# A mixture-of-experts kernel: five experts in the 128-row form and three in the 64-row form, where there were four and four

## The chip, the core and the metric

The kernel runs on one core of one Trainium2 chip. The metric is device time in microseconds (us) of one execution; the kernel before takes 2024.12 us, the median of three runs (2022.58 to 2025.73). All arithmetic is fp32. A product that has to be accurate to fp32 is made of cheaper products of parts: each operand is split into a high part (rounded to `float32r`, by a copy) and a low part (what the rounding left, by a subtraction).

## The reference

Two blocks run one after the other on a sequence of 256 tokens with 1024 features. The first has three attention branches and a feed-forward; the second has two layers, the last of which ends in a mixture of experts. The change touches only this last part:

```
logits = h @ w_router                      # 8 experts
top_val, top_idx = lax.top_k(logits, 2)    # each of 256 tokens goes to 2 experts
gates = softmax(top_val)
y_e = (silu(x_e @ w_gate[e]) * (x_e @ w_up[e])) @ w_down[e]   # x_e: the tokens of expert e
out = sum over the 2 experts of gates * y_e
```

Each expert has gate and up matrices of 1024 by 3584 and a down matrix of 3584 by 1024, 44 MB together, so 352 MB for the eight.

## The kernel before

The mixture runs expert by expert, in eight positions, 0 to 7. All weights stream through four slots of 2 MB each (three in `ring`, one in `ring4`), 21 loads per expert, issued by the SyncE queue in `sp_program`; `load` waits until the last piece of the slot's earlier load has been split. Each load is split in two pieces: ScalarE copies a piece to its high part (`split_to` in `act_program`, line 1180), VectorE subtracts to get the low part (`split_to` in `dve_program`, line 1749), into four pairs of buffers (WHB and WLB, WHX and WLX). TensorE then multiplies, and a buffer is free again when TensorE has read it.

An expert's 3584 hidden columns are done in seven chunks of 512, grouped by `steps_of` as (0), (1, 2), (3, 4), (5, 6); the last expert has (0, 1), (2, 3), (4, 5), (6). In each step come the gate pieces, the up pieces, and then the down pieces of the step before (`expert_piece`, `expert_down`). The tokens of an expert are picked by a product with a 0/1 matrix PO (`lists`, `gather`), and its output is put back by another (`combine`). So the down products of an expert's last two chunks stand behind the gate and up of the next expert's chunk 0.

There are two forms of expert, chosen by position:

- **heavy** (128 rows): the tokens' high parts lie in EH, the low parts in EL. Every product takes three matmuls, high by high, high by low and low by high (`mm3`, lines 426 to 428). One turn per chunk is four transposes (line 1036).
- **light** (64 rows): high and low parts lie side by side in the 128 columns of EH, so two matmuls do the same (lines 1008 and 1009 for gate and up, 1054 and 1055 for down). The turn adds the halves and takes 16 small matmuls per chunk (line 1032).

`order` in `dve_program` ranks the experts by how many tokens they got, most first, with expert 0 always at rank 0 because its loads start before the routing is known. RANK says which rank each position takes; EID, the ids in order of rank, is read by the SyncE queue for the addresses of the loads. CAPV is each expert's limit of tokens, 128 for the ranks that are heavy and 64 for the others. If any expert has more than its limit, a second pass (`sp_second`, `pe_second` and others) loads all the weights once more.

Before the change the positions are heavy, light, heavy, light, heavy, light, heavy, light. The order of the work on each engine is fixed when the program is built; engines wait for each other by semaphores.

Of the kernel before, what the change touches and what calls it, by code (L numbers as in the profile page):

```python
# [12 lines left out]
ALU = mybir.AluOpType  # L13
# [7 lines left out]
NE = 8  # L21
# [7 lines left out]
LIM = 128  # L29
LIM_L = 64  # L30


RANK = (0, 4, 1, 5, 2, 6, 3, 7)
LIGHT = (1, 3, 5, 7)
HEAVY = NE - len(LIGHT)


def steps_of(ex):
# [84 lines left out]
def build(nc, I, table, out):  # L123
    ctx = ExitStack()
    with ctx:
# [98 lines left out]
        def sm(n):  # L224
            sm_at[0] += n
            assert sm_at[0] <= 1008
            return SM[:, sm_at[0] - n:sm_at[0]]
# [180 lines left out]
        def pe_program(e):  # L408
# [3 lines left out]
            def room(b):  # L412
                if banks.last[b] is not None:
                    pe.wait_ge(*banks.last[b])
# [555 lines left out]
            def gather(ex, q):  # L970
# [3 lines left out]
                pe.wait_ge(s_hl, 2)  # L974
                light = ex in LIGHT
                for n, src in enumerate((HH, HL)):
# [14 lines left out]
            def expert_piece(kind, ex, cs, k):  # L991
# [3 lines left out]
                at_ = 0 if kind == "gate" else 2  # L995
                if ex not in LIGHT:
                    pe.wait_ge(*banks.out["ga", ex, (k // 2 if two else k), 0])
                pe.wait_ge(*banks.out["ga", ex, (k // 2 if two else k), 1])
                n_kt = 2 if two else 4
                for j in range(n_kt):  # L1000
                    kt = n_kt * k + j
                    for x, c in enumerate(cs):
# [3 lines left out]
                        wh, wl = hi[:, j, CH * x:CH * x + CH], lo[:, j, CH * x:CH * x + CH]  # L1006
                        if ex in LIGHT:
                            e.matmul(PS[b][:, :], EH[:, kt, :], wh, start=(kt == 0), stop=False)  # L1008
# [13 lines left out]
            def expert_turn(ex, c):  # L1022
                n = NCH * ex + c
                i = n % 2
                room(6)
                if ex in LIGHT:
                    pe.wait_ge(s_tab2, 16)
# [11 lines left out]
            def expert_down(ex, c):  # L1039
                i = (NCH * ex + c) % 2  # L1040
                for h2 in range(2):
# [5 lines left out]
                    for jj in range(2):  # L1047
                        j = 2 * h2 + jj
                        xs = slice(128 * j, 128 * j + 128)
                        for q in range(2):  # L1050
                            cs = slice(512 * q, 512 * q + 512)
                            first, end = c == 0 and j == 0, c == NCH - 1 and j == 3
                            if ex in LIGHT:
                                e.matmul(PS[4 + q][:, :], HTH[:, i, xs], hi[:, jj, cs], start=first, stop=False)  # L1054
# [9 lines left out]
            def scatter_lists(ex):  # L1064
# [3 lines left out]
                for tt in range(2):  # L1068
                    e.transpose(PS[7][:, 128 * tt:128 * tt + 128], PO[:, tt, :].bitcast(F32), ident)
                r = RANK[ex]  # L1070
                e.matmul(PS[7][:, 256:257], PO[:, 0, :].bitcast(F32), GR[:, 0, r:r + 1], start=True, stop=False)
# [666 lines left out]
        def dve_program(e):  # L1738
            v = Stream(e, s_dve)
# [210 lines left out]
            for i, w in enumerate((WFG, WRT)):  # L1950
                t = v.step(e.tensor_copy(W8[2 * i][:, :, :], w[:, :, :]))
# [143 lines left out]
            t = v.step(e.tensor_tensor(LBM, L3[:, 0, :], L3[:, 1, :], ALU.max))  # L2095
            v.wait_ge(*t)
            t = v.step(e.tensor_tensor(LBM, LBM, L3[:, 2, :], ALU.max))
# [3 lines left out]
            t = v.step(e.tensor_tensor(LBS, E3[:, 0, :], E3[:, 1, :], ALU.add))  # L2101
            v.wait_ge(*t)
            t = v.step(e.tensor_tensor(LBS, LBS, E3[:, 2, :], ALU.add))
            v.wait_ge(*t)
            t = v.step(e.reciprocal(LBS, LBS))
            v.wait_ge(*t)
            t = v.step(e.tensor_tensor(LB, E3[:, 0, :], LBS, ALU.mult))
# [54 lines left out]
            t = v.step(e.tensor_tensor_scan(flat(CC), flat(RM), flat(LF), 0.0, ALU.mult, ALU.add))  # L2162
# [20 lines left out]
            for tt in range(2):  # L2183
                for g in range(2):
                    v.wait_ge(s_osq, 2 * tt + g + 1)
                    t = v.step(e.tensor_reduce(SS_HG[:, 8 * tt + 4 * g:8 * tt + 4 * g + 4], SQ2[:, tt, 512 * g:512 * g + 512].rearrange("p (h d) -> p h d", h=4), AX.X, ALU.add))
# [3 lines left out]
            for tt in range(2):  # L2190
                for g in range(2):
                    r = root(("hg", tt))
                    ov = OR[:, tt, 512 * g:512 * g + 512]
                    t = banks.out["ho", tt, g]
# [22 lines left out]
            t = v.step(e.tensor_tensor(LP.rearrange("p (a d) -> p a d", a=2), L4[:, :, 0, :], L4[:, :, 1, :], ALU.mult))  # L2217
# [3 lines left out]
            t = v.step(e.tensor_tensor(NL, LE[:, 1:2], LE[:, 0:1], ALU.subtract))  # L2221
# [96 lines left out]
            for tt in range(2):  # L2318
# [3 lines left out]
                t = v.step(e.tensor_tensor(Q4[:, tt], oth, own, ALU.is_equal))  # L2322
                v.wait_ge(*t)
                t = v.step(e.tensor_tensor(Q4[:, tt], Q4[:, tt], tri, ALU.mult))
# [4 lines left out]
            t = v.step(e.tensor_reduce(MK, C4, AX.X, ALU.add))  # L2329
# [12 lines left out]
            def lists(ex):  # L2342
# [6 lines left out]
                for tt in range(2):  # L2349
                    t = e.tensor_scalar(PO[:, tt, :], iota, pos[:, tt, RANK[ex]:RANK[ex] + 1], None, ALU.is_equal)  # L2350
                t.then_inc(s_po, 1)

            def order():

                v.wait_ge(s_one, 2)
                t = v.step(e.memset(NCNT[:, 0:1], 999.0))
                v.wait_ge(*t)
                oth = NCNT.unsqueeze(1).to_broadcast([128, 8, 8])
                own = NCNT.unsqueeze(2).to_broadcast([128, 8, 8])
                v.step(e.tensor_tensor(C4[:, 0], oth, own, ALU.is_gt))  # L2360
                t = v.step(e.tensor_tensor(C4[:, 1], oth, own, ALU.is_equal))
                v.wait_ge(*t)
                t = v.step(e.tensor_tensor(C4[:, 1], C4[:, 1], tri, ALU.mult))
                v.wait_ge(*t)
                t = v.step(e.tensor_tensor(C4[:, 0], C4[:, 0], C4[:, 1], ALU.add))
                v.wait_ge(*t)
                t = v.step(e.tensor_reduce(RNK, C4[:, 0], AX.X, ALU.add))
                v.wait_ge(*t)
                t = v.step(e.tensor_scalar(CAPV, RNK, HEAVY - 0.5, float(LIM - LIM_L), ALU.is_lt, ALU.mult))
                eight = CT[:, C_IOTA:C_IOTA + 8]  # L2370
                t2 = v.step(e.tensor_tensor(C4[:, 0], RNK.unsqueeze(1).to_broadcast([128, 8, 8]), eight.unsqueeze(2).to_broadcast([128, 8, 8]), ALU.is_equal))
                v.wait_ge(*t)
                t = v.step(e.tensor_scalar(CAPV, CAPV, float(LIM_L), None, ALU.add))
                v.wait_ge(*t2)
                t2 = v.step(e.tensor_tensor(C4[:, 1], C4[:, 0], eight.unsqueeze(1).to_broadcast([128, 8, 8]), ALU.mult))
                v.wait_ge(*t2)
                t2 = v.step(e.tensor_reduce(MX8[:, 0, :], C4[:, 1], AX.X, ALU.add))
                v.wait_ge(*t2)
                e.tensor_copy(EID[:, :], MX8[0:1, 0, :]).then_inc(s_perm, 1)
                v.wait_ge(*t)  # L2380
                v.wait_ge(s_rte, 2)
                for src, dst in ((POS, POSR), (G, GR)):
                    if src is G:
                        v.wait_ge(s_gw, 2)
                    for tt in range(2):
                        t = v.step(e.tensor_tensor(Q4[:, tt], C4[:, 0], src[:, tt, :].unsqueeze(1).to_broadcast([128, 8, 8]), ALU.mult))
                    v.wait_ge(*t)
                    for tt in range(2):
                        t = e.tensor_reduce(dst[:, tt, :], Q4[:, tt], AX.X, ALU.add)
                    if src is G:  # L2390
                        t.then_inc(s_gw, 1)
                    else:
                        v.wait_ge(*v.step(t))
                t = v.step(e.tensor_tensor(MX8[:, 1, :], CNT0, CAPV, ALU.subtract))
                v.wait_ge(*t)
                t = v.step(e.tensor_reduce(MOST, MX8[:, 1, :], AX.X, ALU.max))
                v.wait_ge(*t)
                e.tensor_scalar(CNT[:, :], MOST[0:1, :], float(LIM), None, ALU.add).then_inc(s_most, 1)
# [54 lines left out]
            t = v.step(e.tensor_scalar(H[:, :, :], H[:, :, :], ALPHA, None, ALU.mult))  # L2453
# [4 lines left out]
            t = v.step(e.tensor_scalar(E2, E2, 1.0, None, ALU.add))  # L2458
            v.wait_ge(*t)
            t = v.step(e.reciprocal(E2, E2))  # L2460
            v.wait_ge(*t)
            for tt in range(2):
                e.scalar_tensor_tensor(out=G[:, tt, :], in0=LG8[:, tt, :], scalar=E2[:, tt:tt + 1], in1=MK[:, tt, :], op0=ALU.mult, op1=ALU.mult).then_inc(s_gw, 1)
            order()
            before = []
            for ex in range(NE):
# [251 lines left out]
        def sp_program(e):  # L2718
            q = Stream(e, s_pe)

            def source(i):
# [5 lines left out]
                if ex and (kind, at_) == ("gate", (0, 0)):  # L2727
                    q.wait_ge(s_perm, 1)
                    T["expert", ex] = e.value_load(EID[0:1, RANK[ex]:RANK[ex] + 1], min_val=0, max_val=NE - 1)
                w = w[bass.ds(T["expert", ex], 1)] if ex else w[0:1]  # L2730
# [46 lines left out]
        def flat(x):  # L2777
            return x.rearrange("p h n -> p (h n)")
# [56 lines left out]
        NCNT, CNT0, RNK, CAPV = sm(8), sm(8), sm(8), sm(8)  # L2835
# [71 lines left out]
```

## Time and profile before

| what | value |
|---|---|
| median of three runs | 2024.12 us (2022.58 to 2025.73) |
| the profiled execution | 2025.73 us, its span 2023.9 us |
| TensorE, share of the span busy | 94% |
| VectorE, ScalarE | 74%, 60% |
| HBM read | 509.05 MB |
| experts' loads | 56 of gate, 56 of up, 56 of down, 2 MB each |

The span is the time from the first to the last recorded instruction. The mixture starts at about 1081 us, when the first gather runs, and holds the rest of the span. Because the experts repeat one pattern, the best reading is by windows cut at the same place of each expert: here from the last down matmul of one expert to that of the next, which on TensorE fall at about 1219.4, 1325.9, 1446.4, 1553.1, 1673.6 and 1779.9 us. These five windows are the experts at positions 1 to 5. Each holds chunk 0's gate and up of the expert that follows, and not those of its own, which stand in the window before.

### The profile page before, as it was taken

To read this page: it belongs to the slowest core of one execution; us is meant where nothing else is said; L and a number is where in the kernel's file an instruction comes from. 1 tells how busy PE (TensorE), PEld (TensorE's weight loads), DVE (VectorE), ACT (ScalarE), POOL (GpSimd) and SP (SyncE) were. 2 spreads that over 40 slices of the span, in tenths; PEclk is the share of its full clock that TensorE was granted. 3 is DMA by queue.
4 is the path that set the end of the run, shared out by engine and by line. 5 is a ranking of instruction groups with operands and counts; after the bars stand their busy time and mean duration, and the time that the engine had idled before them with its cause. 6 is when DMAs were issued, how large, how long until landed. Compare 5 with 4: busy or idle time off the path is not lost.

```text
span 2023.9 us, 22529 instructions
## 1 busy us (share of the span) xinstructions
PE 1897.2 (94%) x9235; PEld 1560.2 (77%) x9235; DVE 1501.0 (74%) x1431; ACT 1212.2 (60%) x1243; POOL 156.8 (8%) x123
## 2 busy tenths in 40 slices
PE   5999999999998899989878999999999999999994
PEld 4778777888987778877566887788878887788873
DVE  4645456544589754466667889998999989998996
ACT  4554435433563444344435778877888778877883
POOL 1301010000133210031101000000000000000000
PEclk9999999999999999999877999999999999999997
DMA  8433334554532455444234999999999999999992
GB/s 278 145 134 137 125 125 166 208 177 147 187 136 84 146 207 188 145 163 150 83 132 172 381 355 394 409 406 368 362 414 406 377 363 396 409 405 367 372 409 84
DMA packets 154317, 511.62 MB, mean 253 GB/s; under 512 B 4334, under 2 KB 8672, under 8 KB 139872
## 3 DMA queue, kind: packets, MB, share of 16 engines
q1 hardware_dynamic: 151888, 502.91, 65.7%
q0 software_dynamic: 1424, 4.59, 0.8%
q10 hardware_dynamic: 896, 2.62, 0.3%
q8 instruction: 75, 1.23, 0.2%
q14 instruction: 34, 0.28, 0.0%
HBM read 509.05 MB, written 1.05 MB: 252 GB/s over the span
## 4 chain that ended last, share of the span: by engine, by line
PE 72%; DVE 17%; DMA 4%; ACT 3%; issue 3%; POOL 1%; DVEq 0%; SPq 0%; ACTq 0%; POOLq 0%
PE PS L426 19%; PE PS L428 19%; PE PS L427 19%; DVE WLB L1749 6%; DVE WLX L1749 5%; DMA ring<-in_moe_w_down 3%; PE PS L1054 1%; PE PS L1055 1%; ACT WHB L1180 1%; PE PS L987 1%; PE PS L929 1%; DMA ring<-in_w_mem_kv 1%; PE PS L559 1%; DVE AR L2136 1%; PE PS L840 1%
## 5 line engine op out<-in xcount | busy, mean ns | idle before, releaser
L1749 DVE TENSOR_TENSOR WLB<-ring,WHB 128x2048 fp32r<-128x2048 f32 (+1 forms) x344 | 647.6, 1898 | 136.8 <-ACT WHB L1180 136.2
L1180 ACT ACTIVATE WHB<-ring 128x2048 fp32r<-128x2048 f32 (+1 forms) x344 | 534.1, 1561 | 349.6 <-PE PS L428 315.1
L1749 DVE TENSOR_TENSOR WLX<-ring,WHX 128x2048 fp32r<-128x2048 f32 (+1 forms) x216 | 467.6, 2189 | 49.7 <-ACT WHX L1180 49.6
L1180 ACT ACTIVATE WHX<-ring 128x2048 fp32r<-128x2048 f32 (+1 forms) x216 | 393.3, 1837 | 158.4 <-PE PS L428 137.1
L426 PE MATMUL PS<-WHB,XH 128*128 128x512 f32 (+1 forms) x640 | 258.0, 403 | 11.8 <-DVE XL L1800 6.8
L428 PE MATMUL PS<-WHB,XL 128*128 128x512 f32 (+1 forms) x640 | 251.2, 393 | 0.0
L427 PE MATMUL PS<-WLB,XH 128*128 128x512 f32 (+1 forms) x640 | 250.8, 392 | 0.0
L426 PEld LDWEIGHTS PS<-WHB,XH 128*128 128x128 f32 x640 | 123.2, 192 | 38.0 <-issue 11.4
L2575 POOL TENSOR_TENSOR SM<-SM,MH 128x8 f32<-128x8 f32 (+3 forms) x28 | 36.2, 1299 | 1451.7 <-DVE SM L1762 1451.7
L428 PEld LDWEIGHTS PS<-WHB,XL 128*128 128x128 f32 x640 | 122.8, 192 | 26.2
L427 PEld LDWEIGHTS PS<-WLB,XH 128*128 128x128 f32 x640 | 123.0, 192 | 23.8
L426 PE MATMUL PS<-WHX,XH 128*128 128x512 f32 (+1 forms) x240 | 92.3, 384 | 4.7 <-DVE WLX L1749 4.7
L1008 PE MATMUL PS<-WHB,EH 128*128 128x512 f32 x224 | 91.0, 406 | 2.9 <-DVE WLB L1749 2.0
L428 PE MATMUL PS<-WHX,XL 128*128 128x512 f32 (+1 forms) x240 | 91.4, 381 | 0.0
L427 PE MATMUL PS<-WLX,XH 128*128 128x512 f32 (+1 forms) x240 | 91.3, 381 | 0.0
L1008 PE MATMUL PS<-WHX,EH 128*128 128x512 f32 x224 | 89.9, 401 | 0.3
L426 PE MATMUL PS<-WHX,EH 128*128 128x512 f32 x224 | 89.2, 398 | 0.0
L426 PE MATMUL PS<-WHB,EH 128*128 128x512 f32 x224 | 88.5, 395 | 0.0
L426 PE MATMUL PS<-WHB,HTH 128*128 128x512 f32 x224 | 87.9, 392 | 0.0
L428 PE MATMUL PS<-WHB,EL 128*128 128x512 f32 x224 | 87.8, 392 | 0.0
L427 PE MATMUL PS<-WLB,EH 128*128 128x512 f32 x224 | 87.7, 391 | 0.0
L428 PE MATMUL PS<-WHX,EL 128*128 128x512 f32 x224 | 87.7, 391 | 0.0
(398 smaller groups left out, 3538.7 us busy)
## 6 DMA issues: line engine op xcount, KB each, us to landing
ring<-in_moe_w_gate SPq DMA_DIRECT2D x56, 2048.0 KB, 10.5
ring<-in_moe_w_up SPq DMA_DIRECT2D x56, 2048.0 KB, 11.0
ring<-in_moe_w_down SPq DMA_DIRECT2D x56, 2048.0 KB, 11.0
ring<-in_w_in SPq DMA_DIRECT2D x13, 2048.0 KB, 8.1
ring<-in_hg_w_in SPq DMA_DIRECT2D x8, 2048.0 KB, 8.4
ring<-in_da_w_in SPq DMA_DIRECT2D x6, 2048.0 KB, 8.1
ring<-in_w_gate SPq DMA_DIRECT2D x5, 2048.0 KB, 8.7
ring<-in_w_up SPq DMA_DIRECT2D x5, 2048.0 KB, 7.8
```

The source lines that it names most:

```text
L426: e.matmul(o, xh, wh, start=start, stop=False)
L427: e.matmul(o, xh, wl, start=False, stop=False)
L428: return e.matmul(o, xl, wh, start=False, stop=stop)
L559: e.matmul(PS[2][:, a0:a1], q_[o:o + 64, j, 128 * qt:128 * qt + 128], k_[o:o + 64, j, 0:n], start=True, stop=False)
L840: t = e.matmul(PS[b][:, 128 * j:128 * j + 128], a_k[:, h, 128 * s_t:128 * s_t + 128], a_q[:, h, 128 * t_t:128 * t_t + 128], start=True, st ...
L929: e.matmul(PS[b][:, a0:a1], QD[o:o + 64, h, 128 * qt:128 * qt + 128], KD[o:o + 64, h, 0:n], start=True, stop=False)
L987: t = e.matmul(PS[b][:, 128 * j:128 * j + CAP], src[:, tt, 128 * d:128 * d + 128], PO[:, tt, :], start=(tt == 0), stop=(tt == 1))
L1008: e.matmul(PS[b][:, :], EH[:, kt, :], wh, start=(kt == 0), stop=False)
L1054: e.matmul(PS[4 + q][:, :], HTH[:, i, xs], hi[:, jj, cs], start=first, stop=False)
L1180: e.activation(hi, src, ACT.Copy).then_inc(s_hi, 1)
L1749: e.tensor_tensor(lo, src, hi.bitcast(F32), ALU.subtract).then_inc(s_lo, 1)
L2575: e.tensor_tensor(RR[name], RV[name], MH[:, 0:RR[name].shape[1]], ALU.pow).then_inc(s_rs, 1)
```

## The change

Two tables and one constant are edited. Positions 1, 4 and 7 are now light (1, 3, 5, 7 before), so the order of forms is heavy, light, heavy, heavy, light, heavy, heavy, light. RANK is permuted so that the five heavy positions take ranks 0 to 4 and the three light ones 5, 6 and 7. The comparison that gives each expert its limit of tokens has 4.5 in place of HEAVY - 0.5, which was 3.5, and the name HEAVY is gone.

```diff
-RANK = (0, 4, 1, 5, 2, 6, 3, 7)
-LIGHT = (1, 3, 5, 7)
-HEAVY = NE - len(LIGHT)
+RANK = (0, 5, 1, 2, 6, 3, 4, 7)
+LIGHT = (1, 4, 7)
...
-                t = v.step(e.tensor_scalar(CAPV, RNK, HEAVY - 0.5, float(LIM - LIM_L), ALU.is_lt, ALU.mult))
+                t = v.step(e.tensor_scalar(CAPV, RNK, 4.5, float(LIM - LIM_L), ALU.is_lt, ALU.mult))
```

Since one line is gone, every line number of the changed kernel behind it is one lower. The first place is TensorE where position 2 (heavy) hands over to position 3. Before, EH and HTH are high parts of tokens and hidden values, and PO is the 0/1 matrix; the gather is in the light form:

```order
L426 MATMUL PS<-WHB,EH 128x512
L427 MATMUL PS<-WLB,EH 128x512
L428 MATMUL PS<-WHB,EL 128x512
L985 MATMUL PS<-PO,XH 128x64 x8
L985 MATMUL PS<-PO,XL 128x64 x8
L426 MATMUL PS<-WHX,HTH 128x512
```

In the changed kernel the same place reads:

```order
L425 MATMUL PS<-WHB,EH 128x512
L426 MATMUL PS<-WLB,EH 128x512
L427 MATMUL PS<-WHB,EL 128x512
L986 MATMUL PS<-PO,XH 128x128 x8
L986 MATMUL PS<-PO,XL 128x128 x8
L425 MATMUL PS<-WHX,HTH 128x512
```

The gather has the same number of matmuls and moves 128 columns in each instead of 64. A little later, where chunk 0 of position 3 starts, each weight tile was used twice before:

```order
L427 MATMUL PS<-WLB,HTH 128x512
L428 MATMUL PS<-WHB,HTL 128x512
L1008 MATMUL PS<-WHX,EH 128x512
L1009 MATMUL PS<-WLX,EH 128x512
L1008 MATMUL PS<-WHX,EH 128x512
```

and is now used three times:

```order
L426 MATMUL PS<-WLB,HTH 128x512
L427 MATMUL PS<-WHB,HTL 128x512
L425 MATMUL PS<-WHX,EH 128x512
L426 MATMUL PS<-WLX,EH 128x512
L427 MATMUL PS<-WHX,EL 128x512
```

Over the whole program TensorE gets 168 matmuls of 128x512 more (8088 after 7920), 60 of 128x128 more (1525 after 1465) and 88 of 128x64 fewer (312 after 400).

The second engine is VectorE, at the same handover from position 2 to position 3. Before, after the list PO of the next expert, it splits pieces (WLB, WLX) and finishes two products of gate and up (HID):

```order
L2350 TENSOR_SCALAR PO<-CT,SM 128x128 x2
L1749 TENSOR_TENSOR WLB<-ring,WHB 128x2048
L2420 TENSOR_TENSOR HTL<-PS,HTH 128x512
L1749 TENSOR_TENSOR WLX<-ring,WHX 128x2048 x2
L2427 TENSOR_TENSOR HID<-PS,HID 128x512 x2
L1749 TENSOR_TENSOR WLB<-ring,WHB 128x2048 x2
L1749 TENSOR_TENSOR WLX<-ring,WHX 128x2048 x2
```

Now two copies of the tokens' low parts to EL stand between the splits:

```order
L2349 TENSOR_SCALAR PO<-CT,SM 128x128 x2
L1748 TENSOR_TENSOR WLB<-ring,WHB 128x2048
L2419 TENSOR_TENSOR HTL<-PS,HTH 128x512
L1748 TENSOR_TENSOR WLX<-ring,WHX 128x2048 x2
L2426 TENSOR_TENSOR HID<-PS,HID 128x512 x2
L1748 TENSOR_TENSOR WLB<-ring,WHB 128x2048
L2405 CAST EL<-PS 128x512
L1748 TENSOR_TENSOR WLB<-ring,WHB 128x2048
L1748 TENSOR_TENSOR WLX<-ring,WHX 128x2048
L2405 CAST EL<-PS 128x512
```

The order of the loads in the SyncE queue is the same; only the expert that a position's loads fetch is another one.

## Rows read from the trace of the kernel before

**Rows 1.** The page: share of busy time, TensorE's granted clock and bandwidth in 40 slices.

```profile
PE 1897.2 (94%) x9235; PEld 1560.2 (77%) x9235; DVE 1501.0 (74%) x1431; ACT 1212.2 (60%) x1243; POOL 156.8 (8%) x123
...
PEclk9999999999999999999877999999999999999997
...
GB/s 278 145 134 137 125 125 166 208 177 147 187 136 84 146 207 188 145 163 150 83 132 172 381 355 394 409 406 368 362 414 406 377 363 396 409 405 367 372 409 84
```

**Rows 2.** Windows, positions 1 to 5: us, then PE, PEld, DVE, ACT, POOL, clock, DMA.

```profile
1219.40:1325.90 106.50, 103.16 (x512) 84.01 (x511) 102.36 (x69) 90.43 (x73) 0.00 (x0) 1.00 1.02 402
1325.90:1446.40 120.50, 120.50 (x563) 100.64 (x562) 108.23 (x67) 89.93 (x62) 0.00 (x0) 1.00 0.98 376
1446.40:1553.10 106.70, 103.34 (x513) 84.04 (x512) 102.24 (x69) 90.47 (x73) 0.00 (x0) 1.00 1.02 404
1553.10:1673.60 120.50, 120.50 (x563) 100.65 (x562) 108.23 (x67) 89.93 (x62) 0.00 (x0) 1.00 0.97 375
1673.60:1779.90 106.30, 103.03 (x511) 83.88 (x510) 102.21 (x69) 90.56 (x73) 0.00 (x0) 1.00 1.02 404
```

**Rows 3.** Groups by line, PE, window of position 2 (heavy): xcount, busy us, mean ns, idle.

```profile
L426 PE MATMUL PS<-WHX,EH 128*128 128x512 f32 x48 | 19.2, 400 | 0.0
...
L426 PE MATMUL PS<-WHB,HTH 128*128 128x512 f32 x32 | 12.6, 393 | 0.0
...
L1036 PE MATMUL PS<-CT,HID 128*128 128x128 f32 x28 | 4.4, 280 | 0.0
...
L985 PE MATMUL PS<-PO,XL 128*128 128x64 f32 x16 | 2.1, 277 | 0.0
```

**Rows 4.** Groups by line, PE, window of position 3 (light).

```profile
L1008 PE MATMUL PS<-WHB,EH 128*128 128x512 f32 x48 | 19.8, 413 | 0.9 <-DVE WLB L1749 0.7
...
L1032 PE MATMUL PS<-CT,UB 128*128 128x64 f32 x56 | 7.7, 281 | 0.0
...
L987 PE MATMUL PS<-PO,XH 128*128 128x128 f32 x16 | 2.1, 273 | 1.1 <-DVE HTH L2417 1.1
```

**Rows 5.** Timeline of PE: start us, us, instruction. Heavy turn; then light matmuls and turn.

```profile
1328.64 0.63 PE L1036 MATMUL PS<-CT,HID 128*128 128x128 f32 x4
...
1329.34 0.39 PE L427 MATMUL PS<-WLB,EH 128*128 128x512 f32 x1
...
1446.47 0.39 PE L1008 MATMUL PS<-WHX,EH 128*128 128x512 f32 x1
...
1448.29 1.04 PE L1032 MATMUL PS<-CT,HID 128*128 128x64 f32 x8
...
1450.40 0.39 PE L1009 MATMUL PS<-WLX,EH 128*128 128x512 f32 x1
```

**Rows 6.** Windows, halves of the heavy position 2, then of the light position 3.

```profile
1326.00:1372.00 46.00, 46.00 (x210) 38.16 (x209) 42.77 (x26) 35.07 (x26) 0.00 (x0) 1.00 1.01 403
1372.00:1446.00 74.00, 74.00 (x353) 62.06 (x352) 64.96 (x40) 54.76 (x37) 0.00 (x0) 1.00 0.95 360
1446.00:1470.00 24.00, 23.14 (x105) 17.88 (x104) 23.23 (x16) 21.18 (x17) 0.00 (x0) 1.00 1.00 379
1470.00:1553.00 83.00, 80.50 (x410) 66.44 (x409) 79.31 (x55) 69.19 (x57) 0.00 (x0) 1.00 1.02 411
```

**Rows 7.** Waits in the heavy window of position 2: us in total, times, longest.

```profile
ACT WHX L1180 <- PE PS L428: 14.0, 16, 2.2
...
SPq L2744 <- DVE WLB L1749: 54.1, 11, 6.8
```

**Rows 8.** Waits in the light window of position 3.

```profile
PEld PS L1008 <- DVE WLB L1749: 2.9, 5, 1.1
...
ACT WHB L1180 <- DMA ring<-in_moe_w_up: 2.9, 2, 1.5
```

**Rows 9.** The page: one line's weight loads; issues of the gate weights.

```profile
L426 PEld LDWEIGHTS PS<-WHB,XH 128*128 128x128 f32 x640 | 123.2, 192 | 38.0 <-issue 11.4
...
ring<-in_moe_w_gate SPq DMA_DIRECT2D x56, 2048.0 KB, 10.5
```

## The prediction

> **What bounds the kernel now.** I read the page first, then windows cut expert by expert, then the groups by line inside one heavy and one light window, then the waits of the same two.
>
> The page [rows 1] shows TensorE busy 94% of the span and, from slice 23 on, a bandwidth that swings between 355 and 414 GB/s. That swing is the experts. The changed part alone decides, since nothing before 1081 us is edited.
>
> The five windows [rows 2] show two regimes. A window of a heavy position followed by a light one lasts 120.5 us twice, and TensorE is busy in all 120.50 us of both. A window of a light position followed by a heavy one lasts 106.5, 106.7 and 106.3 us; there TensorE has gaps of some 3.3 us, and VectorE is busy 102.24 of 106.7 us. The granted clock is 1.00 (the level of 2.4 GHz) in all five.
>
> That TensorE is busy is not yet a bound, because its matmuls overlap. The pitch is what to read. In the light stretch eight matmuls of 128x512 start from 1446.47 to 1448.29 us, when the turn starts [rows 5]: 1.82 / 8 = 0.2275 us each, though each one's own duration is about 0.39 us. The heavy window can be rebuilt from that pitch. It has 7 chunks x 24 positions x 3 = 504 matmuls for itself, less 16 x 3 for its own chunk 0, plus 16 x 2 for the light successor's: 488 x 0.2275 = 111.0. The turn costs 1329.34 - 1328.64 less one matmul = 0.47 us, seven times (28 transposes in [rows 3]) 3.3. That leaves 6.2 us for 32 gather matmuls, eight combine matmuls and the lists; the combine takes 8 x 0.2275 = 1.8. Nothing is left over for stalls. So a heavy expert goes at TensorE's issue pace.
>
> The other resources confirm it. In the heavy window ScalarE waits on TensorE's reads, 16 times for one pair of buffers [rows 7], and SyncE waits 54.1 us for slots behind one kind of piece alone. Once the slots have filled, the bandwidth falls from 403 to 360 GB/s [rows 6]. The transfers are ahead and idle for want of room.
>
> A light expert is bound elsewhere. After the stock of loads is used up its bandwidth is 411 GB/s [rows 6], ScalarE waits for the transfer and TensorE for the low parts of WLB [rows 8]. VectorE and the transfers share the bound there, TensorE has room. Its own sum is 352 x 0.2275 = 80.1 for the large matmuls, plus seven turns of 1450.40 - 1448.29 less one matmul = 1.88 us, 13.2, plus the same 6.2: 99.5 us against 106.5.
>
> **The change, part by part.**
>
> *One more heavy position.* Let a window end where the expert's last down matmul ends. Before, positions 1 to 5 give light-heavy 106.5, heavy-light 120.5, 106.7, 120.5, 106.3: 560.5 us. After, the pairs are light-heavy (1), heavy-heavy (2), heavy-light (3), light-heavy (4), heavy-heavy (5). Position 6 is heavy followed by the last light one as before, and position 0 is heavy followed by light as before, so both ends stay as they are.
>
> A heavy-heavy window does not occur in the trace. It is the heavy-light window with chunk 0's gate and up of its successor at three matmuls instead of two: 16 more, 16 x 0.2275 = 3.6 us. The gather of the successor is the same count at the same price, 277 ns a matmul for 64 columns [rows 3] and 273 for 128 [rows 4], so nothing. That makes 120.5 + 3.6 = 124.1 us.
>
> After: 106.5 + 124.1 + 120.5 + 106.5 + 124.1 = 581.7. The difference is 21.2 us, all of it on the path, because in heavy windows TensorE has no idle time at all.
>
> The same from the other side: 168 more matmuls of 128x512, 38.2 us; seven light turns replaced by heavy ones, -7 x (1.88 - 0.47) = -9.9; together 28.3 of issue. Of that, 7.0 us (106.5 - 99.5) was the light expert's waiting and small gaps, which vanish with it. 28.3 - 7.0 = 21.3. The two sums are not independent in the pitch but are in the windows; I take 21.3.
>
> *The handover heavy to heavy.* It brings two copies to EL on VectorE between the splits. Queued behind them are the next low parts, for which TensorE waits. VectorE is busy 108.23 of 120.5 us in a heavy window, so it has 12 us of slack for two copies under 0.7 us each, and between the two gathers TensorE now has 24 down matmuls (5.5 us) instead of 16 as cover. I take nothing. The bound above is what a heavy gather waits for after a light expert, 1.1 us [rows 4], twice: +2.2. The bound below is that the third matmul of chunk 0 is hidden, -3.6 twice: -7.3. The sum runs from 14.0 to 23.5.
>
> *What the slots pass on.* A heavy expert ends with its slots full; a second one cannot make them fuller. So the light expert after two heavy ones starts with the same stock as after one. I take nothing there.
>
> *Permuted ranks and the constant.* Same instructions, same loads; nothing. All 56 gate loads of [rows 9] are the first pass, so no expert overflows now. Limits only rise (rank 4 from 64 to 128), and the heavy positions take just the ranks 0 to 4, so no second pass appears.
>
> Two rules of the Trainium skill speak against this reading. Perfetto Trace Analysis, Identifying the Most-Contended Engine, says that matmul busy time is a bad measure of TensorE's headroom and LDWEIGHTS busy share a good one. Here that share is 100.64 / 120.50 = 84% in a heavy window [rows 2], and by the rule some 16% of it, 20 us, would be room in which the new matmuls could hide. The trace does not support it: one load takes 192 ns [rows 9], and 192 / 227.5 is 84% with no gap between matmuls, so 84% is this pattern's ceiling. SBUF — State Buffer, Summary: rules for kernel authors, says to plan with about 358 GB/s from HBM to SBUF; by that 44 MB would take 123 us for either form, and the change would cost nothing. The trace disagrees, with 411 GB/s in [rows 6].
>
> **The rivals.**
>
> *A, bytes set the pace.* All eight experts read the same 352 MB, so if transfers bound the whole stage, the form would not matter: 2024 us, no change. For it: 404 GB/s in light windows. Against it: 360 GB/s and waits for slots in the second half of a heavy one. Chance 2%.
>
> *A2, room on TensorE.* A heavy window has 120.50 - 100.64 = 19.9 us without a weight load. If the expert's third matmuls fitted in there, 1.4 us of cost would be left: 2025.5. For it: that share. Against it: the rebuilt window, in which the pitch of 0.2275 us leaves no gap. Chance 1%. The rule on the share of weight loads, above, is this case; the one on 358 GB/s is A.
>
> *B, the handover gives something back.* If chunk 0 of a heavy successor costs no more than that of a light one (the low end above), the cost is 14.0 us: 2038.1. For it: nothing measured heavy-heavy. Against: 100% busy at a fixed pitch. Chance 5%.
>
> *C, the light experts speed up.* This is the one that ends on the other side. Two heavy ones in a row give VectorE and the transfers time to get ahead; if the three light experts left then ran at TensorE's own sum, each would save 106.5 - 99.5 = 7.0, 21.0 together, and cancel the cost: 2024.4; with the gather's wait of 1.1 us gone in two of them as well, it would come out at 2022. It decides from the point where the stock at the start of a light expert exceeds today's. Against it: the slots are full after 46 us of a heavy expert [rows 6], and there are only four. Chance 2%.
>
> *D, the second pass appears* through a wrong limit: another 352 MB at 404 GB/s, about 870 us more. Chance below 1%.
>
> *E, dearer handovers*, beyond +2.2: something in the new order stalls TensorE, up to three times 1.1 us at each of the two, 2052. Chance 4%.
>
> **How the numbers follow.** The forecast has the remaining 86%. The profiled execution took 2025.73 us, 1.8 beyond its span, and would become 2047.0. The median shown is 2024.12, 1.6 below that execution, and the prediction is made against it: 2024.12 + 21.3 = 2045.4 us. Runs of before spread over 3.2 us. The range of the forecast with its bound above is 2043 to 2048; widened toward B and E it is 2040 to 2050, which leaves out A, A2, C, D and most of B and E. A measurement here can tell about 0.2%, 4 us, from no change: slower by more than that holds for the forecast, B and E, 95%; within it A, A2 and half of C, 3%; faster, the other half of C and what nobody thought of, 2%.
>
> **What would show it.** Right: windows cut at the last down matmul of about 106.5 at positions 1 and 4, 124.1 at 2 and 5, 120.5 at 3, TensorE busy throughout 2, 3 and 5, and 360 GB/s over nearly all of position 3. Wrong: a light window well below 106 (C), a heavy-heavy one of 120.5 (B) or above 127 (E), or gaps on TensorE inside 2, 3 and 5.

## The result and the profile after

| | median of its runs | profiled execution, span |
|---|---|---|
| before, timed beside it | 2024.92 us (2022.58 to 2027.77) | 2025.73, 2023.9 us |
| changed | 2044.62 us (2043.73 to 2046.56) | 2045.65, 2043.9 us |

The ratio is 1.0098, 95% interval 1.0081 to 1.0115: 19.7 us slower, 20.0 us between the spans. The forecast was 2045.4.

The lines of the changed kernel's page that answer to [rows 1]:

```profile
PE 1922.6 (94%) x9319; PEld 1583.1 (77%) x9319; DVE 1507.5 (74%) x1433; ACT 1211.3 (59%) x1229; POOL 158.2 (8%) x123
...
PEclk9999999999999899989778999999999999999997
...
GB/s 275 150 136 127 124 124 166 205 185 169 161 124 83 168 205 203 127 162 165 42 169 231 376 359 404 409 397 352 351 364 366 411 408 387 351 359 363 373 409 75
```

TensorE is busy 25.4 us longer and its share is 94% as before: a share of the whole span says nothing here. The bandwidth now stays at 351 to 366 GB/s for four slices in a row, where two heavy experts stand together.

The windows cut at the last down matmul of each expert say where the time went. This is the changed kernel, positions 1 to 6 and then the rest (us, then PE, PEld, DVE, ACT, POOL, clock, DMA share, GB/s):

```profile
1217.10:1323.50 106.40, 103.07 (x512) 83.97 (x511) 102.33 (x69) 90.58 (x73) 0.00 (x0) 1.00 1.02 405
1323.50:1447.70 124.20, 124.20 (x580) 103.72 (x579) 110.66 (x70) 89.91 (x61) 0.00 (x0) 1.00 0.97 371
1447.70:1568.20 120.50, 120.50 (x563) 100.64 (x562) 106.39 (x66) 89.61 (x61) 0.00 (x0) 1.00 0.95 361
1568.20:1674.00 105.80, 102.83 (x511) 83.97 (x510) 102.11 (x69) 90.40 (x73) 0.00 (x0) 1.00 1.02 404
1674.00:1798.20 124.20, 124.20 (x580) 103.72 (x579) 110.65 (x70) 89.87 (x61) 0.00 (x0) 1.00 0.97 371
1798.20:1927.40 129.20, 128.41 (x595) 106.40 (x594) 115.11 (x70) 97.46 (x66) 0.00 (x0) 1.00 0.96 361
1927.40:2043.90 116.50, 87.98 (x407) 69.11 (x405) 94.26 (x77) 70.91 (x61) 4.90 (x4) 0.87 0.66 264
```

and these are the last two windows of before, which [rows 2] does not hold:

```profile
1779.90:1909.20 129.30, 128.53 (x595) 106.47 (x595) 116.98 (x71) 97.74 (x67) 0.00 (x0) 1.00 0.97 376
1909.20:2023.90 114.70, 85.35 (x407) 67.65 (x405) 94.35 (x77) 70.78 (x61) 4.44 (x4) 0.91 0.66 267
```

Between the ends of the last down matmuls themselves (1217.39 and 1798.31 now, 1219.72 and 1780.11 before) windows 1 to 5 last 580.9 us and lasted 560.4: +20.5. Window 6 has not moved. The rest is 1.8 us longer, at a lower granted clock (0.87 after 0.91); the first edge comes 2.3 us earlier, though the work in front of it is the same. 20.5 + 1.8 - 2.3 = 20.0.

In window 2, which has no counterpart before, ScalarE waits on TensorE's reads even oftener than in [rows 7], and SyncE waits for slots:

```profile
ACT WHX L1179 <- PE PS L427: 16.4, 19, 2.2
...
SPq L2743 <- DVE WLB L1748: 56.1, 11, 6.4
```

and its gate and up products stand in groups of 56 where [rows 3] has 48, six of them, so 48 matmuls for the successor's chunk 0:

```profile
L425 PE MATMUL PS<-WHB,EH 128*128 128x512 f32 x56 | 21.9, 391 | 0.0
```

### The profile page after: what moved, and what is told of

The parts are those of the page before. It is cut to its first block, busy times and chain, and to the rows that moved or that the text cites. A ratio compares the mean times of both kernels' runs of the same rounds, so it can differ in the third digit from the quotient of the medians.

```text
span 2043.9 us, 22687 instructions
## 1 busy us (share of the span) xinstructions
PE 1922.6 (94%) x9319; PEld 1583.1 (77%) x9319; DVE 1507.5 (74%) x1433; ACT 1211.3 (59%) x1229; POOL 158.2 (8%) x123
## 4 chain that ended last, share of the span: by engine, by line
PE 75%; DVE 14%; DMA 4%; ACT 3%; issue 2%; POOL 1%; DVEq 0%; SPq 0%; ACTq 0%; POOLq 0%
PE PS L425 21%; PE PS L427 21%; PE PS L426 21%; DVE WLB L1748 4%; DVE WLX L1748 4%; DMA ring<-in_moe_w_down 3%; PE PS L986 1%; PE PS L1053 1%; PE PS L1054 1%; DMA ring<-in_w_mem_kv 1%; PE PS L928 1%; PE PS L558 1%; ACT WHB L1179 1%; PE PS L1035 1%; DVE AR L2135 1%
## 5 line engine op out<-in xcount | busy, mean ns | idle before, releaser
L425 PE MATMUL PS<-WHB,EH 128*128 128x512 f32 x280 | 111.1, 397 | 0.0
L425 PE MATMUL PS<-WHX,EH 128*128 128x512 f32 x280 | 110.9, 396 | 0.0
L427 PE MATMUL PS<-WHB,EL 128*128 128x512 f32 x280 | 109.7, 392 | 0.0
L427 PE MATMUL PS<-WHX,EL 128*128 128x512 f32 x280 | 109.4, 391 | 0.0
L426 PE MATMUL PS<-WLB,EH 128*128 128x512 f32 x280 | 109.4, 391 | 0.0
L426 PE MATMUL PS<-WLX,EH 128*128 128x512 f32 x280 | 109.0, 389 | 0.0
L425 PE MATMUL PS<-WHB,HTH 128*128 128x512 f32 x240 | 94.3, 393 | 0.0
L427 PE MATMUL PS<-WHB,HTL 128*128 128x512 f32 x240 | 93.5, 390 | 0.0
L426 PE MATMUL PS<-WLB,HTH 128*128 128x512 f32 x240 | 93.4, 389 | 0.0
```

The costliest lines, as they stand in the source:

```text
L425: e.matmul(o, xh, wh, start=start, stop=False)
L426: e.matmul(o, xh, wl, start=False, stop=False)
L427: return e.matmul(o, xl, wh, start=False, stop=stop)
```

## The experiments

The theory to test: a heavy expert costs what TensorE needs to issue it, whatever its neighbours are; a light one costs what VectorE (or the transfers) need. So form, not place, decides a heavy one's price. The median of before drifts between sessions (2024.9 to 2028.3 us), so I compare ratios to before and, above all, windows. A line of a diff that starts or ends with `...` is shortened.

**Six heavy experts.** One heavy more than the change.

```diff
-RANK = (0, 5, 1, 2, 6, 3, 4, 7)
-LIGHT = (1, 4, 7)
+RANK = (0, 6, 1, 2, 3, 4, 5, 7)
+LIGHT = (1, 7)
...
-... e.tensor_scalar(CAPV, RNK, 4.5, ...
+... e.tensor_scalar(CAPV, RNK, 5.5, ...
```

Expected: 

> Six heavy positions and two light: heavy, light, five heavy in a row, light. Theory (a heavy expert costs TensorE's issue pace, whatever stands before it): against the changed kernel one light-heavy and one heavy-light window (106.3 + 120.5) become two heavy-heavy ones (2 x 124.2), so 2044.6 + 21.6 = 2066 us, and no window differs from these sizes. Rival (heavy experts in a row give the light ones a better start, or queue up something): the last light expert's share from 1927.4 us to the end, 116.5 us, gets shorter, or the later heavy windows get longer than 124.2.

Measured: 2066.94 us, ratio 1.0205 (1.0184 to 1.0226), after 1.0098: 1.07%, 21.7 us. All four heavy-heavy windows take 124.1 us; two of them:

```profile
1449.10:1573.20 124.10, 124.10 (x579) 103.66 (x578) 108.75 (x69) 89.64 (x60) 0.00 (x0) 1.00 0.94 355
...
1697.40:1821.50 124.10, 124.10 (x579) 103.65 (x578) 108.73 (x69) 89.64 (x60) 0.00 (x0) 1.00 0.93 355
```

The price is the same for the next heavy expert. A heavy expert with four heavy ones around it is as fast as one of two. The light window at position 1 took 108.6 us, at a granted clock of 0.98 (see the last section). The last light expert's stretch took 113.8 us (116.5 in the changed kernel, 114.7 before), which one could read as a better start after five heavy ones. But from the edge to the end of TensorE's last long wait it took 83.8 us in both this and the changed kernel; the difference lies in the 16 down matmuls behind that wait, and there it is the clock (last section).

**Two matmuls in place of three at the handover.** Chunk 0 of positions 3 and 6 leaves out the tokens' low parts, so the changed kernel's two heavy-heavy windows hold 16 matmuls fewer each.

```diff
-                        if ex in LIGHT:
+                        if ex in LIGHT or ex in (3, 6) and cs == (0,):
                             e.matmul(PS[b][:, :], EH[:, kt, :], wh, start=(kt == 0), stop=False)
```

Expected: 

> The changed kernel, but in chunk 0 of the heavy experts at positions 3 and 6 (the successors in the two heavy-heavy windows) gate and up take two matmuls instead of three: it leaves out the product of the tokens' low parts there. 2 x 16 matmuls of 128x512 fewer. Theory: 2 x 3.6 = 7.3 us faster than the changed kernel, 2037.3, both heavy-heavy windows at 120.5 instead of 124.1. Rival (the third matmul hides behind splits, weight loads or transfers): no change, windows stay at 124.1.

Measured: 2038.74 us, ratio 1.0063 (1.0039 to 1.0087). 0.35% under the change is 7.1 us, though the two intervals just overlap; the windows are what decides. Both fall from 124.2 to 120.5:

```profile
1323.20:1443.70 120.50, 120.50 (x564) 100.66 (x563) 109.49 (x69) 89.47 (x61) 0.00 (x0) 1.00 0.96 371
1670.50:1791.00 120.50, 120.50 (x563) 100.67 (x562) 109.45 (x69) 89.52 (x61) 0.00 (x0) 1.00 0.98 375
```

Sixteen matmuls fewer save 3.6 us in each, 0.226 us a matmul: each is paid with its pitch and nothing hides. Rival B and rival A2 have fallen.

**Half the bytes for the heavy experts.** Each load of positions 2, 3, 5 and 6 fetches the first half only and leaves old values in the rest of the slot, so the output is not the layer's; the same edit with `in LIGHT` serves the two kernels with half loads below.

```diff
-                e.dma_start(slot(i)[:, 0:t * n].rearrange("p (t n) -> p t n", t=src.shape[1]), src).then_inc(s_ring[SLOT[i]], 16)
+                dst = slot(i)[:, 0:t * n].rearrange("p (t n) -> p t n", t=src.shape[1])
+                if WL[i][2] is None and int(WL[i][0].split()[1]) in (2, 3, 5, 6):
+                    dst, src = dst[:, 0:dst.shape[1] // 2, :], src[:, 0:src.shape[1] // 2, :]
+                e.dma_start(dst, src).then_inc(s_ring[SLOT[i]], 16)
```

Expected: 

> The changed kernel, but each weight load of the heavy experts at positions 2, 3, 5 and 6 brings only half of its bytes, 88 MB less in all (the other half of a slot keeps old values). Theory (heavy experts are bound by TensorE, and their slots are full long before their end anyway): no change, within 1 us, windows 124.1, 120.5, 124.1. Rival A (bytes set the pace): 88 MB at 404 GB/s are 218 us; even a tenth of it would be 22 us faster.

Measured: 2042.51 us, ratio 1.0082 (1.0054 to 1.0111), which overlaps the change's. Two of the windows:

```profile
1320.70:1444.90 124.20, 124.20 (x580) 103.73 (x579) 110.66 (x70) 89.91 (x61) 0.00 (x0) 1.00 0.53 184
1444.90:1565.40 120.50, 120.50 (x563) 100.62 (x562) 106.40 (x66) 89.61 (x61) 0.00 (x0) 1.00 0.63 227
```

At 184 GB/s instead of 371 not a tenth of a microsecond is gained. For the heavy windows rival A has fallen; the light ones are the next question. The profiled span is still 5.5 us shorter than the change's, where I expected at most 1: 3.3 of it lie before the first edge, which the edit does not reach, and 3.0 behind position 6, while windows 1 to 5 are together 0.8 longer.

**Half the bytes for the light experts** of the changed kernel.

Expected: 

> The changed kernel, but each weight load of the light experts (positions 1, 4, 7) brings only half of its bytes. It asks whether a single light expert between heavy ones is bound by VectorE or by bytes. VectorE: its windows of 106.3 and 105.8 us stay within 0.5 us, and only the last one, which has no heavy expert behind it, may gain 1 to 2. Bytes: the windows fall to TensorE's own sum of 99.5 us, 6 to 7 us each, some 15 to 20 us in all.

Measured: 2039.04 us, ratio 1.0060 (1.0040 to 1.0080), 0.38% under the change. The windows of positions 1 and 4:

```profile
1215.60:1321.00 105.40, 102.80 (x512) 83.92 (x511) 101.84 (x69) 90.45 (x73) 0.00 (x0) 1.00 0.71 253
1565.70:1671.10 105.40, 102.74 (x511) 83.96 (x510) 101.84 (x69) 90.46 (x73) 0.00 (x0) 1.00 0.70 253
```

They get 1.0 and 0.4 us shorter, the first by more than my 0.5 but neither by 6 to 7, so bytes do not bind a light expert between heavy ones. TensorE's own sum of 99.5 us is not reached either. What is left is VectorE, busy 101.84 of 105.40 us: every wait of TensorE in the window of position 4 that ends on another engine ends on a VectorE result, mostly a low part, and none on a transfer. The largest group is

```profile
PEld PS L1007 <- DVE WLX L1748: 2.9, 5, 1.1
```

No run took work off VectorE, so this last step is read from the trace and not shown by an edit.

Behind position 6, 116.5 us became 112.5, more than I expected (1 to 2). Of the 4.0 us, 1.4 are the clock in the last 16 down matmuls (last section). The other 2.6 lie in the 83.8 us in front of them; but half the bytes for the heavy experts, with the last expert's own loads whole, shows 2.0 of them as well, so I cannot call them bytes.

**The same four and four, in two groups.** Heavy at 0 to 3, light at 4 to 7.

```diff
-RANK = (0, 5, 1, 2, 6, 3, 4, 7)
-LIGHT = (1, 4, 7)
+RANK = (0, 1, 2, 3, 4, 5, 6, 7)
+LIGHT = (4, 5, 6, 7)
...
-... e.tensor_scalar(CAPV, RNK, 4.5, ...
+... e.tensor_scalar(CAPV, RNK, 3.5, ...
```

Expected: 

> Four heavy and four light as before the change, but in two groups: heavy at positions 0 to 3, light at 4 to 7. Three heavy-light and three light-heavy windows of before become three heavy-heavy (124.2) and three light-light. Theory V (a light expert is bound by VectorE: busy 102.24 us plus 4.6 us of handoffs in a window of 106.7): a light-light window has no copies to EL and no heavy product of the successor, 106.5 - 2.7 = 103.8 us, so +3 x (3.7 - 2.7) = +3 us against before, 2028. Theory B (without a heavy neighbour to refill the slots, light experts are bound by bytes: 44.04 MB at 411 GB/s = 107.2 us): +3 x (3.7 + 0.7) = +13 us, less up to 3 that the first one takes from full slots, 2035 to 2038.

and the same with half the bytes for its light experts. Expected: 

> The kernel with heavy experts at positions 0 to 3 and light ones at 4 to 7, and each weight load of a light expert brings only half of its bytes (the other half of the slot keeps old values). Theory V (VectorE bounds light experts): like the same kernel with full loads, within 1 us each, about 2028. Theory B (bytes): 9 to 10 us faster than with full loads, light-light windows fall from 107 to VectorE's 103.8.

Measured: 2036.54 us, ratio 1.0059 (1.0037 to 1.0081), and with half the bytes 2025.29, ratio 0.9999 (0.9989 to 1.0009). Here is grouping with full loads, light windows 4, 5 and 6:

```profile
1588.10:1693.30 105.20, 101.76 (x496) 81.81 (x494) 100.09 (x66) 89.25 (x74) 0.00 (x0) 0.98 1.02 405
1693.30:1800.10 106.80, 101.45 (x494) 80.45 (x494) 102.34 (x67) 90.95 (x75) 0.00 (x0) 1.00 1.02 411
1800.10:1917.50 117.40, 110.89 (x526) 87.59 (x526) 111.30 (x71) 99.23 (x79) 0.00 (x0) 0.99 1.02 411
```

and with half loads:

```profile
1588.80:1691.00 102.20, 99.46 (x496) 80.69 (x494) 99.77 (x66) 90.38 (x74) 0.00 (x0) 1.00 0.62 208
1691.00:1796.30 105.30, 101.91 (x494) 81.81 (x495) 102.09 (x67) 91.22 (x75) 0.00 (x0) 0.98 0.61 210
1796.30:1909.80 113.50, 109.96 (x526) 87.69 (x526) 110.92 (x71) 99.41 (x81) 0.00 (x0) 0.98 0.61 213
```

Grouping costs 0.59%, 12 us, and with half the bytes all of that is gone. Not all of it need be the grouping's: half loads for three light experts of the changed kernel gave 0.38% too, mostly behind position 6. But here the windows themselves shrink, and with full loads ScalarE waits 15.5 us for transfers in window 5, with half loads not at all. So theory B holds for light experts in a row: without a heavy neighbour that refills the slots, 411 GB/s is the pace, 106.8 us in the first window without a stock (107.2 expected). Between heavy ones VectorE is the pace. The earlier experiment and this one agree: the same expert has two bounds, by its neighbours. The windows account for 3.0, 1.5 and 3.9 us of the 9.7 between the two spans; the second and third half-load windows have a granted clock of 0.98, so they are no clean measure of VectorE's pace.

**Three heavy experts.** Heavy at 0, 3 and 6; run twice.

```diff
-RANK = (0, 5, 1, 2, 6, 3, 4, 7)
-LIGHT = (1, 4, 7)
+RANK = (0, 3, 4, 1, 5, 6, 2, 7)
+LIGHT = (1, 2, 4, 5, 7)
...
-... e.tensor_scalar(CAPV, RNK, 4.5, ...
+... e.tensor_scalar(CAPV, RNK, 2.5, ...
```

Expected: 

> Three heavy positions (0, 3, 6) and five light, limits of tokens set to match (128 for ranks 0 to 2). Against before, windows 1 to 5 are light-light, light-heavy, heavy-light, light-light, light-heavy instead of light-heavy, heavy-light, light-heavy, heavy-light, light-heavy. Theory V: 2 x 103.8 + 2 x 106.5 + 120.5 = 541.1 against 560.5, -19.4 us: 2005. Theory B: a pair of light experts is bound by its bytes less what lies in the full slots, about 214 us together where V has 210.3: -12 us, 2012. If an expert had more than its limit the second pass would show as hundreds of us more.

For the second run: 

> The kernel with heavy experts at positions 0, 3 and 6 once more, as the companion of the next one: about 2012 us, 14 us under before.

Measured: 2012.24 us, ratio 0.9937 (0.9918 to 0.9956), and 2013.11, ratio 0.9929 (0.9907 to 0.9951). Its page still shows 56 loads of gate weights, so the second pass did not run with these inputs: no expert of rank 3 or above has more than 64 tokens. Windows 1, 2 and 3 of the first run:

```profile
1216.20:1320.20 104.00, 100.19 (x496) 80.49 (x494) 100.00 (x66) 89.22 (x74) 0.00 (x0) 1.00 1.02 402
1320.20:1429.90 109.70, 104.22 (x511) 83.92 (x512) 104.65 (x70) 92.36 (x74) 0.00 (x0) 1.00 1.02 411
1429.90:1550.40 120.50, 120.50 (x563) 100.63 (x562) 108.25 (x67) 89.85 (x62) 0.00 (x0) 1.00 0.97 374
```

The first light expert takes 104.0, VectorE's pace (103.8 expected), and lives on full slots. The second takes 109.7 where a single one takes 106.4, at 411 GB/s: bytes. The sum of both, 213.7, is theory B's 214; the second pair, windows 4 and 5, took 214.9. In the second run the pairs took 214.2 and 217.3, the latter with a window of 114.0 us at a granted clock of 0.97. Going from four heavy experts to three thus gives 0.63 and 0.71%, less than the 0.98% of going from five to four, since the second light expert of each pair waits for bytes.

**Three heavy experts, placed at 0, 2 and 5.** RANK is (0, 3, 1, 4, 5, 2, 6, 7) and LIGHT (1, 3, 4, 6, 7).

Expected: 

> Heavy experts at positions 0, 2 and 5: the pairs are heavy-light, light-heavy, heavy-light, light-light, light-heavy, heavy-light, light-light. From the windows measured so far: 106.4 + 120.5 + 104.0 + 109.7 + 120.5 and a last light-light one of 113 to 117 (113.5 with half loads, 117.4 with full ones and no stock), 674 to 678 us against 678.4 for positions 0, 3 and 6, so 0 to 4 us faster than that. Theory (bytes bind a light expert only once the full slots are used up): 115, 2009 us. Rival (the last light expert too lacks bytes, since two light ones end the kernel): the stretch behind the last window gets longer by what the window saves, 2012.

Measured: 2013.39 us, ratio 0.9936 (0.9914 to 0.9959), the same as the other placing within the interval. The windows add to 676.9 us for 1 to 6, but the stretch behind them takes 117.2:

```profile
1779.50:1892.20 112.70, 109.15 (x527) 87.71 (x525) 108.79 (x70) 97.00 (x78) 0.00 (x0) 0.98 1.01 406
1892.20:2009.40 117.20, 85.40 (x406) 66.31 (x406) 96.64 (x78) 72.70 (x62) 4.46 (x4) 0.92 0.68 274
```

against 114.7 before. Up to the end of TensorE's last long wait it was 87.5 us, where the first placing took 83.0; the last 16 down matmuls took 3.9 us against 5.5, at the higher clock, and hid part of that. The rival had it: what the last but one light expert gains from full slots, the last one pays. No gain over the first placing.

**Only the ranks.** Before, with RANK = (0, 7, 3, 4, 1, 5, 2, 6): other experts at the same positions.

Expected: 

> The kernel before with its ranks permuted inside each form (light positions take ranks 7, 4, 5, 6, heavy ones 0, 3, 1, 2), nothing else: other experts at the same positions. Theory (the ids only change addresses): no change, 2024 to 2026 us, all windows as before. Rival (where an expert's weights lie, or how many of its rows are real, matters): any window off by more than 1 us.

Measured: 2024.59 us, ratio 0.9989 (0.9975 to 1.0003): no change. Two windows:

```profile
1321.30:1441.80 120.50, 120.50 (x563) 100.63 (x562) 108.24 (x67) 90.24 (x62) 0.00 (x0) 1.00 0.98 375
1441.80:1549.20 107.40, 103.24 (x511) 83.97 (x511) 102.22 (x69) 90.33 (x73) 0.00 (x0) 1.00 1.02 402
```

Heavy windows agree to 0.1 us. The light ones of positions 3 and 5 are 0.8 and 1.6 us longer than before (107.4, 107.9), one of them more than my bound of 1 us, the latter with ScalarE waiting up to 2.3 us at a time for a load. Whether the place of the weights does that or the execution, one profile can't say; the median shows nothing of it.

## Why the prediction was right

**The bound of a heavy expert.** TensorE's pitch of 0.2275 us was the right thing to read. Heavy-heavy, unseen before the change, was forecast at 124.1 us and took 124.1 to 124.2 in every kernel that has it; heavy-light was forecast unchanged at 120.5, and is, with half the bytes as well as with full ones. That the third matmul is paid in full was shown by taking it out. Weight loads fill 103.72 of 124.20 us in a heavy-heavy window, 84% as in the heavy-light one, so that share was this pattern's ceiling and not room. Window 3 ran at 361 GB/s, as forecast.

**The sum.** Forecast +21.3, measured +20.5 in the windows and +19.7 in the medians. The 0.8 us lies in the light windows: 106.3 and 105.8 us stand where I took 106.5. The second comes after two heavy experts, but among all kernels the window of a single light expert spreads from 105.8 to 108.9 us, so I do not read it as a gift of the slots. Of the remaining 0.8 between windows and medians, 0.5 is what the ends of the two profiled executions do, which the forecast left at nothing: 2.3 us less before the first edge and 1.8 more behind position 6. That they nearly cancel is luck; the end of the first edge's matmul falls between 1214.1 and 1219.7 us in kernels that are the same up to there. It is luck too that 2045.4 lies 0.8 from the measured 2044.62: before, timed again beside it, came out 0.8 higher than the 2024.12 that the forecast started from, and in the difference the forecast is 1.6 off.

**The handover.** Forecast at nothing, between -7.3 and +2.2; it was nothing. TensorE is busy throughout, 124.20 of 124.20 us, with the two copies to EL among the splits. The prediction took the gather's price from the mean duration of a matmul (277 and 273 ns), which overlaps the next one's and is not what TensorE pays; the starts agree, though: 16 gather matmuls took 1.70 us with 64 columns and 1.73 with 128.

**The slots.** Forecast: nothing is passed on. Right for one against two heavy experts. The statement that VectorE and the transfers share the bound of a light expert was too loose: halving the bytes takes the transfers out between heavy ones, where VectorE is what is left, and the transfers bind in a row of light ones. The change makes no such row, so the sum did not need it.

**Ranks and limits.** Nothing, as forecast; permuting the ranks alone changed no median beyond its interval, and no second pass ran.

**The rivals.** A fell by the half loads, A2 and B by the handover with two matmuls. C, quicker light experts, fell with the windows of position 4 (105.8, not 99.5). D did not occur. E would have needed gaps in windows 2 and 5, and there are none. The chances hold one slip: A, A2 and half of C are 4% by the prediction's own figures, not 3%, and what is left for faster is 1%.

## What to carry to other kernels

Price a change of form in a repeated pattern by windows cut at the same instruction of each repeat, and by the pitch of the engine that never rests; the shares of the whole span stayed at 94%. If two forms have different bounds (here issue on one side, VectorE and bytes on the other), alternate them, since the slots fill up again while the slow-issuing one runs: grouping the same experts cost 12 us. And a form that is chosen for the worst case should be counted against the data: three heavy experts are enough for these inputs, 0.6 to 0.7% under before, with the second pass as the guard for other inputs.

## What the runs showed of the hardware

The granted clock of TensorE falls to its lower level (1.2 GHz) inside some light experts, and not in the same one each time. In the run with two matmuls at the handover, the light window at position 1 took 108.9 us instead of 106.3. The changed kernel has no such dip there. These are that window and two stretches in it:

```profile
1214.30:1323.20 108.90, 104.97 (x512) 85.11 (x511) 102.50 (x69) 90.47 (x73) 0.00 (x0) 0.98 1.01 400
1290.00:1295.00 5.00, 5.00 (x19) 4.04 (x19) 5.00 (x4) 3.56 (x4) 0.00 (x0) 0.66 1.05 387
1295.00:1300.00 5.00, 5.00 (x32) 4.45 (x31) 4.73 (x4) 3.72 (x4) 0.00 (x0) 1.00 1.04 421
```

The stretch at 0.66 has 19 matmuls and the next at 1.00 has 32. It lies just behind TensorE's wait before the gather of the next expert ([rows 4] has such a wait, 1.1 us), here 1.14 us. These are rows from there on:

```profile
1288.68 1.08 PE L986 MATMUL PS<-PO,XH 128*128 128x128 f32 x8 [1.14 <-DVE HTH L2416]
...
1292.04 0.63 PE L1053 MATMUL PS<-WHB,HTH 128*128 128x512 f32 x1
1292.47 0.63 PE L1054 MATMUL PS<-WLB,HTH 128*128 128x512 f32 x1
...
1294.88 0.39 PE L1053 MATMUL PS<-WHB,HTH 128*128 128x512 f32 x1
1295.11 0.39 PE L1054 MATMUL PS<-WLB,HTH 128*128 128x512 f32 x1
```

At the lower clock the matmuls start 0.43 us apart, at the higher one 0.23. In the run with six heavy experts the clock falls behind the same wait, and TensorE was busy 3.88 of the 5 us up to 1294. But the changed kernel has the same wait there, 1.17 us, with TensorE busy 3.83 of 5 us, and its clock stayed at 1.00; so the wait alone does not decide it. With such a dip the window took 108.6 and 108.9 us. Without one it took 105.8 to 107.9, so a dip costs some 2.5 us against the same kernel's typical 106.3. The 107.4 and 107.9 of the permuted ranks had a clock of 1.00 and stay unexplained. No heavy window had a dip.

The last expert shows what the clock costs more cleanly. TensorE waits 1.93 us for the last chunk's hidden values (HTH) and then runs the last 16 down matmuls. The changed kernel, and then the one with six heavy experts:

```profile
2011.40 0.77 PE L1053 MATMUL PS<-WHX,HTH 128*128 128x512 f32 x1 [1.93 <-DVE HTH L2416]
2011.96 0.63 PE L1054 MATMUL PS<-WLX,HTH 128*128 128x512 f32 x1
2012.39 0.63 PE L1053 MATMUL PS<-WHX,HTH 128*128 128x512 f32 x1
```

```profile
2034.78 0.47 PE L1053 MATMUL PS<-WHX,HTH 128*128 128x512 f32 x1 [1.93 <-DVE HTH L2416]
2035.09 0.40 PE L1054 MATMUL PS<-WLX,HTH 128*128 128x512 f32 x1
2035.32 0.39 PE L1053 MATMUL PS<-WHX,HTH 128*128 128x512 f32 x1
```

After the same wait, 14 of the 16 were slow (over 0.5 us long) in the changed kernel, 7 before and none with six heavy experts, and the 16 took 6.7, 5.3 and 3.9 us. Of the 1.8 us by which the rest of the changed kernel was longer than before, 1.4 lie here, 0.3 in front of the wait and 0.1 behind the last down matmul.
